# Expert choice of two tiles in the query stage, 112 candidates a head, batched one-hot tiles, gates stored by chunk blocks, and three places of the first block

## The reference

```python
# retention output, per head: y -> (y - mean) * rsqrt(var + EPS) * gain
# experts ("peer"), per block of 128 tokens:
q = (hb @ w_q).reshape(T, PEER_HEADS, 2, PEER_HALF)        # 8 heads, 2 halves of 128
s = jnp.einsum('thpc,hpnc->thpn', q, sub_keys)             # 128 keys a half
sub_s, sub_i = lax.top_k(s, K)                             # K = 16: the first level
cand = (sub_s[:, :, 0, :, None] + sub_s[:, :, 1, None, :]).reshape(T, PEER_HEADS, K * K)
top_s, top_i = lax.top_k(cand, K)                          # the second level
k1 = jnp.take_along_axis(sub_i[:, :, 0], top_i // K, axis=-1)
k2 = jnp.take_along_axis(sub_i[:, :, 1], top_i % K, axis=-1)
expert = k1 * PEER_N_KEYS + k2                             # of 128 * 128 = 16384
g = jax.nn.softmax(top_s.astype(jnp.float32), axis=-1)
act = jax.nn.gelu(jnp.einsum('td,thkd->thk', hb, expert_u[expert]), approximate=False) * g
return jnp.einsum('thk,thkd->td', act, expert_v[expert])
```

## Time and profile before

| | us |
|---|---|
| median of 3 runs | 3749.82 (3744.86 to 3751.38) |
| profiled execution | 3745.25, span 3743.3 |
| PE busy | 3531.6 (94%) |
| DVE busy | 2139.0 (57%) |
| ACT busy | 1400.0 (37%) |
| POOL busy | 690.7 (18%) |
| mean granted clock | 0.971 of full speed |

### The profile page before, as it was taken

The page is one execution under the profiler, slowest core; times in us unless marked ns, Lnnn a source line. Parts: engine busy times, 40 slices in busy tenths (PEclk is TensorE's granted clock), DMA queues, the critical chain, the costliest instruction groups (busy, mean ns, idle before and its releaser), DMA issues.

```text
span 3743.3 us, 54637 instructions
## 1 busy us (share of the span) xinstructions
PE 3531.6 (94%) x21337; PEld 3035.9 (81%) x21337; DVE 2139.0 (57%) x4570; ACT 1400.0 (37%) x2283; POOL 690.7 (18%) x645
## 2 busy tenths in 40 slices
PE   7999998988999998999998999999999979999997
PEld 5877886878989898999996668867888855777886
DVE  3353443398989766888886365265333255537443
ACT  3232323323545453333334354154212345526222
POOL 0000000004889783543331000000000000000000
PEclk8999999999999999999998999999999989999998
DMA  6224233366878789999995101101112211220232
GB/s 223 96 79 147 90 100 120 131 218 237 302 270 295 270 307 339 374 372 363 370 369 183 40 29 52 63 23 40 63 63 68 90 63 40 68 79 29 96 99 93
DMA packets 220416, 594.50 MB, mean 159 GB/s; under 512 B 17793, under 2 KB 101377, under 8 KB 215809
## 3 DMA queue, kind: packets, MB, share of 16 engines
q1 hardware_dynamic: 156592, 380.68, 29.6%
q0 software_dynamic: 36864, 134.23, 9.9%
q10 hardware_dynamic: 26704, 76.09, 5.4%
HBM read 530.11 MB, written 60.82 MB: 158 GB/s over the span
## 4 chain that ended last, share of the span: by engine, by line
PE 81%; DVE 11%; DMA 3%; ACT 2%; issue 2%; ACTq 0%; POOL 0%; SPq 0%; DVEq 0%
PE bank L756 58%; PE bank L974 13%; PE bank L1066 2%; PE bank L1052 2%; PE bank L941 2%; DVE WL L1554 2%; PE bank L780 1%; PE bank L834 1%; DMA WR<-in_weights 1%; DVE rows L1857 1%; DMA WR<-in_vrows 1%; DVE hotA L1886 1%; DVE Rw L1826 1%; DVE SrowA L2053 1%; PE bank L867 0%
## 5 line engine op out<-in xcount | busy, mean ns | idle before, releaser
L1554 DVE TENSOR_TENSOR WL<-WR,WH 128x1024 fp32r<-128x1024 f32 x512 | 630.5, 1233 | 815.7 <-ACT WH L1158 758.3
L1158 ACT ACTIVATE WH<-WR 128x1024 fp32r<-128x1024 f32 x512 | 536.9, 1057 | 817.3 <-PE bank L974 272.8
L756 PE MATMUL bank<-H2h,WH 128*128 128x512 f32 (+1 forms) x1624 | 577.9, 356 | 4.5 <-DVE H2l L1582 4.5
L756 PE MATMUL bank<-H2h,WL 128*128 128x512 f32 (+1 forms) x1624 | 572.9, 353 | 0.0
L756 PE MATMUL bank<-H2l,WH 128*128 128x512 f32 (+1 forms) x1624 | 572.2, 352 | 0.0
L756 PE MATMUL bank<-Hh,WH 128*128 128x384 f32 (+1 forms) x1440 | 526.4, 366 | 20.5 <-DVE WL L1554 20.5
L756 PE MATMUL bank<-Hh,WL 128*128 128x384 f32 (+1 forms) x1440 | 512.1, 356 | 0.0
L756 PE MATMUL bank<-Hl,WH 128*128 128x384 f32 (+1 forms) x1440 | 511.0, 355 | 0.0
L974 PE MATMUL bank<-ah,WH 128*128 128x384 f32 x1024 | 344.3, 336 | 17.3 <-issue 14.9
L756 PEld LDWEIGHTS bank<-H2h,WH 128*128 128x128 f32 x1624 | 307.1, 189 | 51.9 <-issue 7.7
L974 PE MATMUL bank<-al,WH 128*128 128x384 f32 x1024 | 343.9, 336 | 0.0
(11 more groups left out here) (317 smaller groups left out, 5522.9 us busy)
## 6 DMA issues: line engine op xcount, KB each, us to landing
WR<-in_weights SPq DMA_DIRECT2D x498, 512.0 KB
WR<-in_vrows SPq DMA_DIRECT2D x128, 512.0 KB
gelu_by_expert<-geU ACTq DMA_DIRECT2D x128, 192.0 KB
gates_by_expert<-tab ACTq DMA_DIRECT2D x24, 1024.0 KB
geV<-gelu_by_expert SPq DMA_DIRECT2D x32, 768.0 KB
Gt<-gates_by_expert SPq DMA_DIRECT2D x16, 1536.0 KB
x_kept<-X ACTq DMA_DIRECT2D x2, 3072.0 KB, 9.1
X<-x_kept ACTq DMA_DIRECT2D x2, 3072.0 KB, 10.8
```

What stands on the lines that cost most here:

```text
L756: yield nc.tensor.matmul(b[0:rows, out_cols], a, r, start=n == 0, stop=n == len(pairs) - 1)
L1158: act.activation(WH[:, n % SLOTS, :, :].rearrange("p a b -> p (a b)"), WR[:, c % SLOTS, :, :].rearrange("p a b -> p (a b)"), ACT.Copy)\
L1554: v.tensor_tensor(WL[:, n % SLOTS, :, :].rearrange("p a b -> p (a b)"), WR[:, plan.splits[n] % SLOTS, :, :].rearrange("p a b -> p (a b)"), ...
```

## The change

Six edits. (1) qk: the rotary product is two steps behind its tile and not one, with one modulate a step. (2) The four heads' variances go into one bank, on four groups of 32 partitions, with one root and one reciprocal; four small products ("spread") after g_ret 1 bring them back to 128 rows. (3) Query stage: the product pq f + 1 stands in step f, the wait for the sub-keys comes after `together`, the modulates start at f = 2; and DVE does the first level of tiles 3 and 0 there, one (head, half) a step. (4) `choose` adds only 4 x 16 and 12 x 4 candidates a head, the pairs which can be among 16 largest sums of sorted lists, and computes the indices back from that layout; the look-up's multiply is one instruction and not eight. AHEAD is 8. (5) `hots` on DVE is one compare of 128x512, and ACT multiplies by the gate (`hot_weights`). (6) The gates in DRAM are laid out by blocks of 16 chunks, and two thirds of the first two blocks' gates are loaded before U's chunk 96.

```diff
-AHEAD, STEP = 16, 5
-HOT_AT = {0: 23, 1: 55, 2: 87}
-GATE_AT = {3: 10, 0: 21, 1: 53, 2: 85}
-SOFT_AT = {3: 9, 0: 19, 1: 49, 2: 81}
+AHEAD, STEP = 8, 5
+HOT_AT = {0: 22, 1: 54, 2: 86}
+GATE_AT = {3: 10, 0: 20, 1: 52, 2: 84}
+SOFT_AT = {3: 7, 0: 17, 1: 50, 2: 82}
+PRELOAD_AT = 96
+EARLY = (SPARSE, 0)
+NC1, NC2 = 64, 48
...
-    gates_dram = nc.dram_tensor("gates_by_expert", [NTB, P, NK, TB], f32, kind="Internal").ap()
+    gates_dram = nc.dram_tensor("gates_by_expert", [NK // KPT, P, NTB, KPT * TB], f32, kind="Internal").ap()
...
-                sp.dma_start(Gt[t % 2].rearrange("p n k t -> p n (k t)"),
-                             gates_dram[:, :, KPT * t:KPT * (t + 1), :].rearrange("n p k t -> p n (k t)"))\
+                sp.dma_start(Gt[t % 2][:, n0:n1, :, :].rearrange("p n k t -> p (n k t)"),
+                             gates_dram[t, :, n0:n1, :].rearrange("p n x -> p (n x)"))\
...
-            for n in range(v0 + 2):
+            u0, v0, early = plan.chunk_at[("U", PRELOAD_AT)], plan.chunk_at[("V", 0)], NTB * 2 // 3
+            for n in range(u0):
                 load(n)
-            load_gelu(0)
+            sp.wait_ge(kt_ready, len(DENSE))
+            for t in range(2):
+                load_gelu(t)
+            for b in range(2):
+                sp.wait_ge(g_stored[b], 16 * (early // 2))
+            for t in range(2):
+                load_gates(t, 0, early)
+            for n in range(u0, v0 + 2):
+                load(n)
...
-            for f in range(1, 9):
-                if 2 <= f < 8:
+            for f in range(2, 10):
+                if f < 8:
                     linear(("qk", f), ("qk", f), H1, slice(0, T))
-                pe.wait_ge(act_read, k.reading(act_read, ("qk", f - 1)))
-                product(("qkp", f - 1), slice(0, T), [(consts["perm128"][:, :], R1[:, (f - 1) % 3, :])])
+                pe.wait_ge(act_read, k.reading(act_read, ("qk", f - 2)))
+                product(("qkp", f - 2), slice(0, T), [(consts["perm128"][:, :], R1[:, (f - 2) % 3, :])])
...
-            for h in range(RET_H):
-                pe.wait_ge(ysq_ready, k.next(ysq_ready, 2))
-                product(("var", h), slice(0, T), [(ones[:, :], XW[:, 2 * h + e, :]) for e in range(2)])
+            def variances(b):
+                for e in range(2):
+                    for h in range(RET_H):
+                        yield nc.tensor.matmul(b[QUAD * h:QUAD * (h + 1), :], ones[:, 0:QUAD], XW[:, 2 * h + e, :],
+                                               start=e == 0, stop=e == 1)
...
-            pe.wait_ge(sub_loaded, k.at(sub_loaded, 16))
             for f in range(17):
+                if f == 1:
+                    pe.wait_ge(sub_loaded, k.at(sub_loaded, 16))
                 if f == 0:
                     together([(("pq", g), ("pq", g), slice(0, T)) for g in range(2)], H1)
-                if 2 <= f < 16:
-                    linear(("pq", f), ("pq", f), H1, slice(0, T))
+                if 1 <= f < 15:
+                    linear(("pq", f + 1), ("pq", f + 1), H1, slice(0, T))
...
+            def hot_weights(tt, q):
+                n = tt * (P // 4) + q
+                act.wait_ge(hot_keys, n + 1)
+                for t in range(4):
+                    c = 4 * q + t
+                    hot = hotA[:, n % HOTS, t, :]
+                    act.activation(hot, hot, ACT.Copy, scale=KT[:, tt % 2, 2, c:c + 1]).then_inc(hot_a, k.inc(hot_a))
...
-                    dma(gates_dram[tb, :, :, :].rearrange("p k t -> p (k t)"),
-                        Gs[:, sl, :, :].rearrange("p k t -> p (k t)")).then_inc(g_stored[sl], 16)
+                    dma(gates_dram[:, :, tb, :].rearrange("u p x -> p u x"),
+                        Gs[:, sl, :, :].rearrange("p (u k) t -> p u (k t)", k=KPT)).then_inc(g_stored[sl], 16)
...
                 out_of(("U", b), geU[:, b % 2, :], slice(0, TN), ACT.Gelu)
+                if hot_in(b):
+                    hot_weights(*hot_in(b))
                 if hot_in(b - HOT_LAG):
                     gates_out(*hot_in(b - HOT_LAG))
...
+            for f in range(17):
+                if f:
+                    dve.wait_ge(act_read, act_at(("sc", f - 1)))
+                    first_choice(f - 1)
...
-                for h in range(PH):
-                    yield v.tensor_tensor(cand[:, h, :].rearrange("p (a b) -> p a b", a=PK),
...
+                for c0, na, nb, a0 in ((0, 4, PK, 0), (NC1, 12, 4, 4)):
+                    yield v.tensor_tensor(cand[:, :, c0:c0 + na * nb].rearrange("p h (a b) -> p h a b", a=na),
...
-                    for h in range(PH):
-                        yield v.tensor_tensor(work[:, h * PK:(h + 1) * PK, :], work[:, h * PK:(h + 1) * PK, :],
-                                              tf[:, h, s, :].unsqueeze(1).to_broadcast([P, PK, PK]), ALU.mult)\
-                            .then_inc(dve_step, k.inc(dve_step))
+                    split_ = work.rearrange("p (h j) a -> p h j a", h=PH)
+                    yield v.tensor_tensor(split_, split_, tf[:, :, s, :].unsqueeze(2).to_broadcast([P, PH, PK, PK]),
+                                          ALU.mult).then_inc(dve_step, k.inc(dve_step))
...
-                for t in range(4):
-                    c = 4 * q + t
-                    v.tensor_scalar(hotA[:, n % HOTS, t, :], consts["iota128"][:, :],
-                                    KT[:, tt % 2, 0, c:c + 1], KT[:, tt % 2, 2, c:c + 1],
-                                    ALU.is_equal, ALU.mult).then_inc(hot_a, k.inc(hot_a))
+                v.tensor_tensor(hotA[:, n % HOTS, :, :], consts["iota128"][:, :].unsqueeze(1).to_broadcast([P, 4, P]),
+                                KT[:, tt % 2, 0, 4 * q:4 * q + 4].unsqueeze(2).to_broadcast([P, 4, P]),
+                                ALU.is_equal).then_inc(hot_keys, k.inc(hot_keys))
```

More of the change, by code:

```diff
@@ L189, in make_plan @@
             spreads(("norm1",))
-    for f in range(9):
+    for f in range(10):
         if f < 8:
@@ L194, in make_plan @@
             p.job(("qk", f), "A", [("qk", f)])
[L195 to L199, removed]
+        if f >= 2:
+            p.job(("qkp", f - 2), "V")
+            modulate(MODS[0] + f - 2, MODS[0], MODS[1])
+    modulate(MODS[1], MODS[0], MODS[1])
     rows("v", ("w_in", 1024), "A")
@@ L217, in make_plan @@
             p.job((name, f, "x"), "A", [(name, f)])
+            if name == "g_ret" and f == 1:
+                for h in range(RET_H):
+                    p.job(("spread", h), "V")
             modulate(MODS[1] + m0 + f, MODS[1], MODS[2])
@@ L233, in make_plan @@
     for f in range(17):
-        for g in (() if f in (1, 16) else (0, 1) if f == 0 else (f,)):
+        for g in (0, 1) if f == 0 else (f + 1,) if f < 15 else ():
             p.chunk(("pq", g), ("peer_w_q", 0, g))
@@ L241, in make_plan @@
             p.job(("sc", f - 1), "A")
-        if f < 9:
-            modulate(MODS[2] + f, MODS[2], MODS[3])
+        if 2 <= f < 11:
+            modulate(MODS[2] + f - 2, MODS[2], MODS[3])
     for b in range(NK):
@@ L554, in build @@
             for i_, n_ in enumerate(("cv", "ca", "cb", "kk1", "kk2", "gg", "cpos", "cpa")))
+        top_of = {tt: (tab[:, 2048:2304], tab[:, 2304:2560]) for tt in EARLY[1:]}
+        top_of = {tt: tuple(t_.rearrange("p (i k) -> p i k", k=PK) for t_ in pair) for tt, pair in top_of.items()}
+        Re = {tt: place(f"Re{tt}", F0 + at, 8, P) for tt, at in zip(EARLY, (9216, 10240))}
         gsum, KT = place("gsum", f1 + 1792, 1, 16), place("KT", f1 + 1824, 2, 3, P)
@@ L888, in _ @@
                     linear((name, f, "x"), (name, f), H1, slice(0, T))
+                    if name == "g_ret" and f == 1:
+                        pe.wait_ge(var_ready, k.next(var_ready))
+                        for h in range(RET_H):
+                            p0 = slice(QUAD * h, QUAD * (h + 1))
+                            product(("spread", h), slice(0, T), [(ones[p0, :], ST[p0, 0, 0, :])])
                     modulate(MODS[1] + m0 + f, MODS[1], MODS[2])
@@ L1238, in _ @@
                 dma(dst, d[src][:, :]).then_inc(sgu_loaded, 16)
-            for f in range(8):
-                if f >= 3:
-                    act.wait_ge(dve_read, dve_at(("qkp", f - 3)))
-                out_of(("qk", f), R1[:, f % 3, :], slice(0, T), scale=1.0 if f < 4 else RET_DK ** -0.5)
-                for m in range(0 if f == 1 else f, f + 1 if f else 0):
-                    modulate(MODS[0] + m, MODS[0], MODS[1])
+            for f in range(10):
+                if f < 8:
+                    if f >= 3:
+                        act.wait_ge(dve_read, dve_at(("qkp", f - 3)))
+                    out_of(("qk", f), R1[:, f % 3, :], slice(0, T), scale=1.0 if f < 4 else RET_DK ** -0.5)
+                if f >= 2:
+                    modulate(MODS[0] + f - 2, MODS[0], MODS[1])
             for pair in range(4):
@@ L1262, in _ @@
                         .then_inc(ysq_ready, k.inc(ysq_ready))
-            for h in range(RET_H):
```

(2 more changed lines are left out.)

133 lines of the change are left out of this document (91 added, 42 removed).

## The result

| | before | after |
|---|---|---|
| median | 3748.27 us (4 runs, 3744.86 to 3751.38) | 3777.14 us (4 runs, 3771.23 to 3781.03) |
| ratio | | 1.0076, 95% interval 1.0058 to 1.0093 |
| profiled execution, span | 3745.25, 3743.3 | 3781.03, 3779.3 |

What follows compares the result with a forecast made beforehand. TensorE was taken as the bound, busy 3531.6 of 3743.3 us, so only its waits could shrink. Gains of 89.7 against a hot-stage stall of 107 gave +17, 3766 us, range 3680 to 3825.

Steps and rivals of the forecast that it cites:

- The circle: Hot stage, blocks 22 to 117: ACT and DVE wait for each other in every block, 5.2 us, 5.5 with a modulation.
- The hold D: Hot stage, every fourth block: the new gates store holds the gelu store's issue on ACT's queue, 3.7 us, bounds 0.44 to 6.9.
- the lead of 5.65: Hot stage: the engines' lead over PE, in us, used up once for each of three tiles, −17 us of stall.
- The heavy step: Blocks 49 and 81: five 2.29 us DVE operations of the choice for tiles 1 and 2 cost 9.5 each, 19 together.
- U0 to U20: First U blocks: cheaper choosing on DVE cuts PE's lost time from 33.7 us to 3.8, a gain of about 30.
- 1.6 at each tile and 2.0 at gg: U0 to U20: PE losses expected to stay beside six 2.29 us DVE operations in one step, less 1.4 of clock.
- qk: Early qk steps: the rotary product two steps late gives PE work during the load and ACT's copy, gain about 7 us.
- it adds 0.6 at the end: End of the qk loop: the later rotary product costs 0.6 us, subtracted from that term's gain.
- Variance, query stage: Variance: one reciprocal replaces four, gain 14.5 us; query stage: shorter sub-key and load waits and moved modulates, gain 9.6.
- Early loads: Two thirds of V's gates loaded before U96: gain 10 us between U and V, price 0, at most 3.
- The signs named ahead: Changed profile: gelu issues of 2 to 5 us, WL waits every fourth block totalling 100, smaller waits where gains were forecast.
- Rival 1: Hot stage: ACT's queue takes the gates store whole, hold 0.44, stall 28.7, result 3689 us, faster; chance 0.22.

Runs made afterwards that it cites:

- experiment eight: Changed kernel with one-hot tiles by DVE alone (3706), plus empty steps between the look-up's six heavy operations, AHEAD 9, STEP 6: 3700.2 us, ratio 0.9869.
- experiment nine: Changed kernel with one-hot tiles by DVE alone (3706), plus early loads apart, look-up's heavy operations apart, old order of qk steps: 3690.1 us, ratio 0.9854.
- experiment seven: Kernel before (3749) with only the early gelu and gates loads added ahead of U's chunk 96, old gates layout: 3749.3 us, ratio 0.9996.
- experiment one: Changed kernel (3777) with the old layout of the gates in DRAM, stores and loads; early loads stay: 3736.8 us, ratio 0.9969.
- two: Changed kernel (3777) with the gates store issued behind the gelu store of the same block: 3723.2 us, ratio 0.9935.

## Why the prediction was right, and where it wasn't

- **The circle and its length: right.** Forecast 5.2 a plain block and 5.5 with a modulation; the trace has 5.0 to 5.2 and 5.2 to 5.4. PE waits for WL behind ACT about once in a four and not evenly: six times in the 170 us of 1040 to 1210, 9.0 us together, 2.3 the longest. The four multiplies take 1.28 together and were taken as 1.2.
- **The hold D: the mechanism right, the size too large.** Forecast 3.7, measured 2.75 in the mean. The sum that it gives is right all the same: blocks 24 to 48 lost 22.2, 56 to 80 19.9, 96 to 120 17.2, 3.3 a four; the forecast's 24 × (0.53 + 3.7) less 17 of lead is 3.5 a four. That is luck in part. D is 1 lower; the lead of 5.65 that was to absorb something in each tile isn't seen in the stretches; the late landing of gelu stores was left out; and so was the clock: the forecast priced waits alone, while 23 of the stretch's 84 us are PE busy for longer.
- **The page's rule.** The Trainium skill (DMA: Bandwidth & Descriptors, section Anatomy of one DMA — SWDGE (gpsimd) path) calls descriptor generation small, and says that many can be emitted before the cost shows; it is written for GpSimd's path. By it D would be 0.44. On ACT's queue the medians are 2.31 behind 2048 runs, 0.59 behind 1024 and 0.47 behind 128: that agrees for the two smaller ones alone.
- **The heavy step: right where it was looked for, missed where it was priced low.** Tiles 1 and 2: blocks 48 to 56 and 80 to 88 each take 6.6 to 6.9 longer than before, of which the two fours' 3.3 are all; so the new lump costs what the old wait did, as forecast (9.5 + 1.7 against 10.1 and 8.5):

```profile
1009.01 1.22 DVE L1590 TENSOR_TENSOR WL<-WR,WH 128x1024 fp32r<-128x1024 f32 x1
...
1010.87 2.34 DVE L1916 TENSOR_TENSOR Rw<-Rw,topf 128x2048 f32<-128x2048 f32 x1
1013.25 2.29 DVE L1919 TENSOR_REDUCE kk<-Rw 128x128 f32<-128x2048 f32 x1
...
1020.22 2.29 DVE L1919 TENSOR_REDUCE kk<-Rw 128x128 f32<-128x2048 f32 x1
...
1023.56 1.22 DVE L1590 TENSOR_TENSOR WL<-WR,WH 128x1024 fp32r<-128x1024 f32 x1
```

  From one low split (1009.01) to the next (1023.56) are 14.5 us, and PE waits 8.0 of them. The multiply over 128x2048 takes 2.34 and 2.29, taken as 2.29.
- **U0 to U20: the term that failed.** Forecast −30, measured −15.3 over blocks 0 to 24. The step that failed is "1.6 at each tile and 2.0 at gg": the lumps of tiles 3 and 0 cost 13 more than that, as experiment eight shows. I had let PE's distance of two blocks absorb them, and not counted that after such a wait the weights' loads, which wait for PE, start late as well. The prediction's own sign came, too: waits for WL in 700 to 870 are 11.2 us, above the 10 at which it called the term wrong. The chain behind the first lump has one that takes 9.84 while four rows' gathers run (DMA share 1.02 in 770 to 780), with PE's own work before it:

```profile
766.40 4.58 PE bank L771 x26
...
771.99 9.84 DMA WR<-in_weights
```

  How much of these 13 is the gathers' was not separated.
- **qk: failed.** Forecast −7, measured about +1.6 (Vr at 120.72 and 119.08). The first wait did go, but the step "it adds 0.6 at the end" was wrong: the last two steps of the lagged loop have no product of a weight tile, so PE runs through them and waits for v's weights, whose slots come free with the modulation chunks, now later:

```profile
99.06 0.57 PE bank L849 x16
99.63 0.33 PE bank L771 x2
...
100.06 4.34 DMA WR<-in_weights
...
104.47 1.07 ACT WH L1184
```

  Undone in experiment nine, Vr is at 118.98.
- **Variance, query stage: right.** To norm 2 the gain is 13.4, and with qk's 1.6 taken out 15.0, forecast 14.5. To U0 it is 8.7, forecast 9.6.
- **Early loads: the gain right, the price wrong.** −11.0 behind block 120, forecast −10. But "0, at most 3" for 3.5 MB ahead of the weights was 5 to 7 (blocks 88 to 96 take 11.6 longer, two fours are 6.6; 6.6 longer in experiment seven). In seven it is the weights that are late, as the term had it. The look-ahead of 21 us was counted as if SP had four free slots, but a load there waits for the split of the chunk four back. In the changed kernel it is another queue: just behind the early loads, with the DMA engines full (share 1.03 in 1295 to 1305), comes the longest of the 24 held gelu issues, and ACT's next high split waits 9.50 for it.

```profile
1295.53 8.93 ACTq L1351 DMA_DIRECT2D gelu_by_expert<-geU  x1
1304.59 1.06 ACT L1184 ACTIVATE WH<-WR 128x1024 fp32r<-128x1024 f32 x1 [9.50 <-issue]
```

  The term had not asked what a full set of DMA engines does to ACT's queue.
- **The signs named ahead: most came.** Of the 24 gelu issues, 13 take 2 to 5 us, 9 less than 2 (none under 1.21) and 2 more. PE's waits for WL in 870 to 1450 are 24 with 58.8 us, where 100 were named. No wait is left in the variance window, and 4.5 before V.

In the traces the forecast of +17 became +36: qk gave 8.6 less than forecast, U0 to block 24 gave 15 less, the early loads cost 5 more, and the rest of the hot stage cost 9 less. Rival 1, 3689, did not come. It is near what the kernel takes once the circle is taken away (3706) and the lumps are apart (3690), which was not its reason; with its own condition, short issues, the kernel takes 3737 in experiment one and 3723 in two.

The layout, which the text ahead calls blocks of 16 chunks, is 16 blocks of 8 chunks; the run of 512 B and their number are as stated.

## What to carry to other kernels

Before giving one engine a part of another's step, draw who waits for whom in the same pass of the loop: if A's first work in a pass feeds B and B's feeds A's last, the look-ahead no longer helps, and whatever delays A once is paid in full by the end of the chain. Price a transfer by how many runs it has on an engine's queue and by what is issued right behind it; putting the large store behind the urgent small one gained 54 us here, and undoing the layout 40. A loop whose steps are lagged has passes at its end in which work is missing that hid the loads; look at these first.

## What the runs showed of the hardware that was not expected

Behind 2048 runs of 512 B the next issue on ACT's queue took 2.31 us (median), behind 1024 runs 0.59, behind 128 of 8 KB 0.47: more a step than a slope. It also depends on what else the DMA engines move: the longest, 8.93 and 12.37, stand just behind the early loads. A hold of 3.71 us in the mean, 24 times, did not show in the time where the engine had two blocks of lead: 3706.3 with it and 3707.1 without. That isn't quite nothing, since each of these two kernels loses some 8 us in blocks 88 to 96, the one by its longest hold and the other without any: 49.9 and 50.4, where it was 42.4.
